# The opening of a two-block transformer on one core: raw input transposed and projected first, its norm factor applied to the sums

## The chip, the cores and the metric

The kernel runs on one NeuronCore of a Trainium2 chip. The metric is device microseconds of one execution, here the median of several. The core's engines work from queues of their own and wait for each other by semaphores: TensorE (PE: matrix products into PSUM; its weight loads are shown apart as PEld), VectorE (DVE), ScalarE (ACT), GpSimd (POOL) and SyncE (SP, which here only issues transfers). An engine takes its instructions strictly in the order in which the program gives them.

## The reference, cut to what matters

Two blocks follow one another on 256 tokens of width 1024. The first begins with a norm and one wide projection, and the change lies wholly in these lines:

```
def rmsnorm(x, g):
    xf = x.astype(jnp.float32)
    y = xf * lax.rsqrt(jnp.mean(xf * xf, axis=-1, keepdims=True) + EPS)
    return (y * g.astype(jnp.float32)).astype(x.dtype)
...
h = rmsnorm(x, norm_mix_g[l])
proj = h @ w_in[l]
cb, cc, ch, sq, sk, sv, rq, rk, rv, rg, gate_logits = jnp.split(proj, SPLIT_POINTS, axis=-1)
```

So each token (a row of x) has one factor, 1/sqrt(mean square + EPS), and each of the 1024 columns one gain g. sq, sk and sv (512 columns each) are query, key and value of a stick-breaking attention. All that follows (retention, gates, cross attention, two MLPs, an SSD mixer, an attention with latent keys) is the same program before and after.

## The kernel before

All products are exact to float32 by splitting. A value is rounded to a short part ("hi", type fp32r) and the rest ("lo" = value - hi), and a product is three matmuls: hi·hi, hi·lo, lo·hi. Weights come from memory in **units** of 128 x 2048 elements (1 MB) through five buffers. For each unit ACT makes `whi` from `raw` (helper `hi()`, L830), DVE makes `wlo` from both (helper `lo()`, L1310), and PE may begin a unit's third kind of product only when its `lo_split` count is reached; `weights(u)` (L2117 and after) waits for it at the unit's beginning. A buffer is loaded again when PE has finished the unit five places earlier. In this text unit 0 and unit 1 are the two halves of sq, unit 2 and unit 3 those of sk, unit 4 and unit 5 those of sv (each the product over one half of the 1024 inputs), and unit 6 is the first of the retention's. The places of `hi()` and `lo()` in ACT's and DVE's programs are written out by hand; nothing plans them at run time. PE's own order is unit after unit.

The opening before: SP loads token tile 0 of x and the two halves of unit 0; ACT loads tile 1, the identity matrix and the gains. DVE gets the mean square of tile 0 (bn_stats), ACT that of tile 1 (L871). GpSimd takes both to the power -0.5 (L742), DVE and ACT scale a tile each (L1531, L876) into `xs`, PE transposes it (L2286), and ACT and DVE make `h_hi` and `h_lo` from the transposed tile, times the gains (L864, L1364). PE fills the time until then with 20 products of zeros (L2325). It then runs `first_unit` (unit 0: hi·hi, L2295, then L2299 with `wlo`, L2304 with `h_lo`) and `second_unit` (unit 1), then unit 2 and so on (L2125 to L2127). Behind its `lo()` of unit 4 DVE computes the angles of a rotary table (L1548 to L1562) and zeroes two halves of the key buffers (L1564, L1565), and then takes the `lo()` of units 5, 6 and 7.

PSUM has eight banks; a bank is claimed by PE when its last content is `drained`.

Of the kernel before, what the change touches and what calls it, by code (L numbers as in the profile page):

```python
# [221 lines left out]
def plan(w):  # L222
# [4 lines left out]
    p.transposes("h1", 4, (4, 5, 6, 7))  # L227
    SQ, SK, SV, RET, CB, CC, CH, GATE = (MIX * j for j in (3, 4, 5, 6, 0, 1, 2, 10))
# [254 lines left out]
def build(nc, w, out):  # L483
# [3 lines left out]
    with ctx:  # L487
# [71 lines left out]
        squares, g_rows = room(6272, D), room(7552, P)[0:KD, :]  # L559
        xs = room(8320, NT, D)  # L560
# [48 lines left out]
        g_mix_in, squared = sem("g_mix_in"), sem("squared")  # L609
        x_scaled = [sem(f"x_scaled{t}") for t in range(NT)]  # L610
        first_in, first_hi, zeroed = sem("first_in"), sem("first_hi"), sem("zeroed")
        ms_ready, rstd_ready = sem("ms_ready"), sem("rstd_ready")
# [101 lines left out]
        def _(pool):  # L714
# [24 lines left out]
            pool.wait_ge(pool_step, 1)  # L739
            powers[0] += NT  # L740
            pool.wait_ge(ms_ready, NT)
            nc.gpsimd.tensor_tensor(rstd[:, 0:NT], ms[:, 0:NT], mhalf[:, 0:NT], ALU.pow).then_inc(rstd_ready, NT)  # L742
# [70 lines left out]
        def _(act):  # L813
# [53 lines left out]
            act.dma_start(xn[:, 1, :], w["x"][0].rearrange("(t p) n -> p t n", p=P)[:, 1, :]).then_inc(x_in[1], 16)  # L867
            act.dma_start(ident, w["constants"][:, C_IDENT:C_TRI]).then_inc(ident_in, 16)
            act.dma_start(g_rows, w["norm_mix_g"][0].rearrange("(k p) -> k p", p=P)).then_inc(g_mix_in, 16)
            act.wait_ge(x_in[1], 16)  # L870
# [9 lines left out]
            copy_bank(pv[:, G_MIX:G_MIX + KD], "g_mix", lambda b: b[:, 0:KD])  # L880
            wait_drained(act, "g_mix")
            for j in range(4):
                scaled_part_bank(h_hi[:, 2 * j:2 * j + 2, :], ("h1", j), G_MIX + 2 * j)
# [3 lines left out]
            for name in ("sq", "sk"):  # L887
                for j in range(2):
                    hi()
                    if name == "sq":  # L890
                        copy_bank(sqT[:, 2 * j:2 * j + 2, :], (name, j), pair)
                    else:
                        b = wait_bank(act, (name, j))
                        A(skT[0][0:64, 2 * j:2 * j + 2, :], pair(b)[0:64], ACT.Copy)
                        A(skT[1][64:P, 2 * j:2 * j + 2, :], pair(b)[64:P], ACT.Copy).then_inc(drained[use[(name, j)][0]], 1)
# [9 lines left out]
            for t in range(NT):  # L905
                copy_bank(svN[:, t, :], ("sv", t), lambda b: b[:, :])
# [384 lines left out]
        def _(dve):  # L1291
# [234 lines left out]
            dve.wait_ge(squared, 1)  # L1526
            V.tensor_scalar(ms[:, 1:2], msq[:, 1:2], 1.0 / D, RMS_EPS, ALU.mult, ALU.add).then_inc(ms_ready, 1)
            powers[0] += 1
            wait_inverse(NT)
            for c in halves:  # L1530
                V.tensor_scalar(xs[:, 0, c], xn[:, 0, c], rstd[:, 0:1], None, ALU.mult).then_inc(x_scaled[0], 1)  # L1531
# [6 lines left out]
            wait_drained(dve, "g_mix")  # L1538
# [26 lines left out]
            V.memset(skT[1][0:64, :, :], 0.0).then_inc(sk_zeroed, 1)  # L1565

# [542 lines left out]
        def _(pe):  # L2109
# [169 lines left out]
            def first_unit():  # L2279

                h1 = [claim(("h1", j)) for j in range(4)]
                for t in range(NT):
                    for k in range(KD):
                        if k % 4 == 0:
                            pe.wait_ge(x_scaled[t], k // 4 + 1)
                        last = nc.tensor.transpose(h1[k // 2][:, T * (k % 2) + P * t:T * (k % 2) + P * t + P], xs[:, t, P * k:P * k + P], ident)  # L2286
                        if t == 1 and k % 2:
                            last.then_inc(fill(("h1", k // 2)), 1)
                b = claim(("sq", 0))
                for k in range(KD):  # L2290
                    if k % 4 == 0:
                        pe.wait_ge(hi_split if k else first_hi, 1)
                    pe.wait_ge(x_hi, k + 1)
                    for c in range(2):
                        M(b[:, T * c:T * c + T], view(whi[0], KD, 256)[:, k, P * c:P * c + P], h_hi[:, k, :], start=(c, k) == (0, 0), stop=False)  # L2295
                w_hi, w_lo, _, _ = weights(at[("sq", 0)])
                for k in range(KD):
                    for c in range(2):
                        M(b[:, T * c:T * c + T], w_lo[:, k, P * c:P * c + P], h_hi[:, k, :], start=False, stop=False)  # L2299
                for k in range(KD):  # L2300
                    if k % 2 == 0:
                        wait_drained(pe, ("h1", k // 2))
                    for c in range(2):
                        last = M(b[:, T * c:T * c + T], w_hi[:, k, P * c:P * c + P], h_lo[:, k, :], start=False, stop=(c, k) == (1, KD - 1))  # L2304
                last.then_inc(unit_used, 1)

            def second_unit():
# [5 lines left out]
                for c in range(2):  # L2313
                    for k in range(KD):
                        for x_ in (h_hi, h_lo):
                            M(b[:, T * c:T * c + T], w_hi[:, k, P * c:P * c + P], x_[:, k, :], start=(c, k) == (0, 0) and x_ is h_hi, stop=False)
                _, w_lo, _, _ = weights(at[("sq", 1)])
                for c in range(2):
                    for k in range(KD):
                        last = M(b[:, T * c:T * c + T], w_lo[:, k, P * c:P * c + P], h_hi[:, k, :], start=False, stop=(c, k) == (1, KD - 1))  # L2320
# [3 lines left out]
            for _ in range(20):  # L2324
# [6 lines left out]
            second_unit()  # L2331
            for name in ("sq", "sk"):
                for j in range(2):
                    if name == "sk":
                        b_unit(at[(name, j)], h_hi, h_lo, one((name, j)))
# [11 lines left out]
            for k in range(2):  # L2347
                a_unit(at[("sv", k)], h_hi, h_lo, 4 * k, banks, k == 0, k == 1)


            pe.wait_ge(cst_a_in, 16)
# [633 lines left out]
```

## Time and profile before

| | us |
|---|---|
| median of 3 runs | 1258.52 (1258.48 to 1260.17) |
| span of the profiled execution | 1257.2 |
| PE busy | 1242.1 |
| DVE busy | 932.5 |
| ACT busy | 684.2 |
| POOL busy | 68.2 |

The span runs from the first to the last instruction of the profiled execution; the median of the timed runs is 1.3 us longer, as it holds what lies around the instructions. Matmuls overlap, so PE's pace is to be read from the distance of starts and not from the duration of one.

### The profile page before, as it was taken

The page shows a single profiled execution, that of the slowest core. Times are in us where ns is not written, and L with a number is a line of the kernel's source. Part 1 is how long each engine was busy: PE and PEld are TensorE (multiplying, and loading weights), DVE is VectorE, ACT ScalarE, POOL GpSimd, SP SyncE. Part 2 cuts the span into 40 slices and gives each one's busy share as a digit, 9 for nine tenths or more (in the row PEclk, how much of TensorE's full clock was granted, in tenths as well). Part 3 has the DMA queues.
Part 4 walks back from the last instruction along what each step waited for, and adds up shares of the span by engine and source line. Part 5 has one row for each costly group of instructions (what it writes and reads, how often), then busy time and mean ns, then how long its engine had stood idle before and what let it go on. Part 6 is the DMA issues. An engine that isn't in the chain of part 4 may idle for free. (4 is left out here: it accounts for less than half of the span.)

```text
span 1257.2 us, 18334 instructions
## 1 busy us (share of the span) xinstructions
PE 1242.1 (99%) x7514; PEld 1102.9 (88%) x7514; DVE 932.5 (74%) x1292; ACT 684.2 (54%) x872; POOL 68.2 (5%) x93
## 2 busy tenths in 40 slices
PE   9999999999999999999999999999999999999997
PEld 8878999989988888889998888888888888888886
DVE  6676857875456666577997998788888868788877
ACT  6654444343553444455777655466655574566652
POOL 2000000100000000000003331000000000000000
PEclk9999999999999999999999999999999999999999
DMA  9664545656435665647656654655554744655551
GB/s 294 219 184 144 185 143 188 214 186 209 168 101 170 199 194 178 197 138 219 185 168 210 203 191 151 217 185 201 184 186 138 231 134 134 201 194 179 197 194 41
DMA packets 162595, 227.97 MB, mean 181 GB/s; under 512 B 7853, under 2 KB 123825, under 8 KB 162384
## 3 DMA queue, kind: packets, MB, share of 16 engines
q1 hardware_dynamic: 159392, 216.68, 53.5%
q0 software_dynamic: 2816, 9.52, 2.3%
q8 instruction: 60, 0.98, 0.3%
q10 hardware_dynamic: 304, 0.59, 0.1%
q14 instruction: 23, 0.19, 0.0%
HBM read 225.68 MB, written 1.10 MB: 180 GB/s over the span
## 5 line engine op out<-in xcount | busy, mean ns | idle before, releaser
L1310 DVE TENSOR_TENSOR wlo<-raw,whi 128x2048 fp32r<-128x2048 f32 (+3 forms) x185 | 415.9, 2260 | 113.9 <-ACT whi L830 112.8
L830 ACT ACTIVATE whi<-raw 128x2048 fp32r<-128x2048 f32 (+3 forms) x185 | 345.9, 1883 | 16.0 <-DMA raw<-in_w_xkv 6.1
L2159 PE MATMUL psum<-h_both,whi 128*128 128x512 f32 x714 | 254.7, 396 | 0.0
L2158 PE MATMUL psum<-h_both,wlo 128*128 128x256 f32 x714 | 199.4, 279 | 0.3 <-DVE h_both L1364 0.3
L2125 PE MATMUL psum<-h_both,whi 128*128 128x256 f32 x688 | 195.9, 285 | 0.0
L2127 PE MATMUL psum<-h_both,wlo 128*128 128x256 f32 x688 | 194.6, 283 | 0.0
L2126 PE MATMUL psum<-h_both,whi 128*128 128x256 f32 x688 | 194.6, 283 | 0.0
L2125 PE MATMUL psum<-whi,r_hi 128*128 128x512 f32 x446 | 176.6, 396 | 0.0
L2127 PE MATMUL psum<-whi,r_lo 128*128 128x512 f32 x446 | 173.9, 390 | 0.0
L2126 PE MATMUL psum<-wlo,r_hi 128*128 128x512 f32 x446 | 173.8, 390 | 0.0
L2159 PEld LDWEIGHTS psum<-h_both,whi 128*128 128x128 f32 x714 | 134.0, 188 | 27.6
L2158 PEld LDWEIGHTS psum<-h_both,wlo 128*128 128x128 f32 x714 | 134.6, 189 | 5.2 <-DVE h_both L1364 0.6
L2125 PEld LDWEIGHTS psum<-h_both,whi 128*128 128x128 f32 x688 | 131.9, 192 | 0.4 <-issue 0.3
L2126 PEld LDWEIGHTS psum<-h_both,whi 128*128 128x128 f32 x688 | 131.9, 192 | 0.2
L2127 PEld LDWEIGHTS psum<-h_both,wlo 128*128 128x128 f32 x688 | 131.9, 192 | 0.0
L2125 PE MATMUL psum<-whi,h_both 128*128 128x512 f32 (+4 forms) x304 | 118.7, 391 | 0.4 <-issue 0.3
L1964 DVE SCALAR_TENSOR_TENSOR arena<-arena,pv 128x256 f32<-128x256 f32 x176 | 77.3, 482 | 51.7 <-ACT arena L1165 43.9
L2127 PE MATMUL psum<-whi,h_both 128*128 128x512 f32 (+4 forms) x304 | 113.5, 373 | 0.0
L2126 PE MATMUL psum<-wlo,h_both 128*128 128x512 f32 (+4 forms) x304 | 113.1, 372 | 0.0
L2127 PEld LDWEIGHTS psum<-whi,r_lo 128*128 128x128 f32 x446 | 83.7, 188 | 17.9
L2126 PEld LDWEIGHTS psum<-wlo,r_hi 128*128 128x128 f32 x446 | 83.9, 188 | 16.5
L2125 PEld LDWEIGHTS psum<-whi,r_hi 128*128 128x128 f32 x446 | 83.8, 188 | 15.3
(350 smaller groups left out, 1807.1 us busy)
## 6 DMA issues: line engine op xcount, KB each, us to landing
raw<-in_ffn_up SPq DMA_DIRECT2D x40, 1024.0 KB, 5.1
raw<-in_w_in SPq DMA_DIRECT2D x31, 1024.0 KB, 5.8
raw<-in_ssd_in_proj SPq DMA_DIRECT2D x22, 1024.0 KB, 5.4
raw<-in_ffn_down SPq DMA_DIRECT2D x22, 1024.0 KB, 4.9
raw<-in_w_up SPq DMA_DIRECT2D x16, 1024.0 KB, 5.6
raw<-in_w_down SPq DMA_DIRECT2D x16, 1024.0 KB, 4.9
raw<-in_w_xkv SPq DMA_DIRECT2D x8, 1024.0 KB, 5.2
raw<-in_ssd_out_proj SPq DMA_DIRECT2D x8, 1024.0 KB, 5.2
```

The lines of the kernel that those rows point to most:

```text
L830: A(whi[u % SLOTS][:, 0:kt * n], raw[u % SLOTS][:, 0:kt * n], ACT.Copy).then_inc(hi_split, 1)
L1310: V.tensor_tensor(wlo[s][:, 0:kt * n], raw[s][:, 0:kt * n], whi[s][:, 0:kt * n].bitcast(F32), ALU.subtract).then_inc(lo_split, 1)
L1964: ins = V.scalar_tensor_tensor(y, fpad[g % 2][x][:, ct, tap:tap + T], pv[:, wcol:wcol + 1], y, ALU.mult, ALU.add)
L2125: M(o, a_hi, b_hi, start=start, stop=False)
L2126: M(o, a_hi, b_lo, start=False, stop=False)
L2127: return M(o, a_lo, b_hi, start=False, stop=stop_)
L2158: M(b[:, 0:T], w_lo_k, h_hi[:, k, :], start=False, stop=False)
L2159: return M(b[:, :], w_hi_k, h_both[:, :, k, :], start=False, stop=k == kt - 1)
```

## The change

- SP loads both tiles of x, one behind the other, ahead of unit 0. ACT loads only the gains and the identity.
- PE transposes the **raw** x as soon as a tile is there (15 products of zeros ahead of it in place of 20), and ACT and DVE make `r_hi` and `r_lo` from it times the gains. sq, sk and sv (units 0 to 5) are computed from these un-normalized values.
- GpSimd rounds the first half of unit 0 (a copy of 128 x 1024), ahead of its constants' loads. The powers come behind eleven of its loads.
- DVE gets the mean squares of both tiles, tile 1's behind the `wlo` of unit 0. Behind `lo()` of unit 2 it makes two diagonal matrices of the tokens' factors. PE multiplies them with a matrix of ones, which gives `factor`, the factors along the free axis in all partitions. ACT copies it out of PSUM bank 2, which unit 2's sums claim next.
- DVE multiplies sq and sk by `factor` as it takes them out of PSUM (before: plain copies by ACT). ACT copies sv with the factor as its scale.
- The normalized h for all later projections is made beside this: DVE writes `xg` = transposed x times gain times factor, ACT rounds it to `h_hi`, DVE takes the rest, `h_lo`. PE waits for that behind unit 5 (`h1_lo`).

The diff, cut to its core:

```diff
 # SP
-            sp.dma_start(xn[:, 0, :], x_tiles[:, 0, :]).then_inc(x_in[0], 16)
+            for t in range(NT):
+                sp.dma_start(xn[:, t, :], x_tiles[:, t, :]).then_inc(x_in[t], 16)
...
 # GpSimd
-            pool.wait_ge(ms_ready, NT)
-            nc.gpsimd.tensor_tensor(rstd[:, 0:NT], ms[:, 0:NT], mhalf[:, 0:NT], ALU.pow).then_inc(rstd_ready, NT)
+            nc.gpsimd.memset(ones, 1.0).then_inc(pool_step, 1)
+            pool.wait_ge(first_in, 16)
+            nc.gpsimd.tensor_copy(whi[0][:, 0:UNIT // 2], raw[0][:, 0:UNIT // 2]).then_inc(first_hi, 1)
...
                 pool.dma_start(pvraw[r0:r0 + src.shape[0], blk, :], src).then_inc(pv_in, 16)
+            pool.wait_ge(pool_step, 2)
+            rsqrt_tiles()
...
 # ACT
-            A(squares, xn[:, 1, :], ACT.Square, accum_out=msq[:, 1:2]).then_inc(squared, 1)
-            act.wait_ge(first_in, 16)
-            A(whi[0][:, 0:UNIT // 2], raw[0][:, 0:UNIT // 2], ACT.Copy).then_inc(first_hi, 1)
-            act.wait_ge(rstd_ready, NT)
-            for c in range(2):
-                A(xs[:, 1, 512 * c:512 * c + 512], xn[:, 1, 512 * c:512 * c + 512], ACT.Copy, scale=rstd[:, 1:2]).then_inc(x_scaled[1], 1)
+            copy_bank(pv[:, G_MIX:G_MIX + KD], "g_mix", lambda b: b[:, 0:KD])
+            wait_drained(act, "g_mix")
+            for j in range(4):
+                scaled_part_bank(r_hi[:, 2 * j:2 * j + 2, :], ("h1", j), G_MIX + 2 * j)
             act.wait_ge(landed[0], 16)
             A(whi[0][:, UNIT // 2:], raw[0][:, UNIT // 2:], ACT.Copy).then_inc(hi_split, 1)
...
                     hi()
...
+                    if (name, j) == ("sq", 1):
+                        copy_bank(factor, "factor", lambda b: b[:, 0:T])
                     if (name, j) == ("sk", 1):
+                        for i in range(4):
+                            wait_drained(act, ("h1", i))
+                            part(h_hi[:, 2 * i:2 * i + 2, :], xg[:, 2 * i:2 * i + 2, :])
...
 # DVE
+            dve.wait_ge(x_in[1], 16)
+            norm_tile(1, xn, RMS_EPS, True)
+            lo()
+            lo()
+            for t in range(NT):
+                wait_inverse(t + 1)
+                V.tensor_scalar(factor_diag[:, P * t:P * t + P], ident, rstd[:, t:t + 1], None, ALU.mult).then_inc(diag_ready, 1)
+            lo()
+            wait_drained(dve, "factor")
+            both_tiles = lambda p0, p1: factor[p0:p1].unsqueeze(1).to_broadcast([p1 - p0, 2, T])
+            for j in range(2):
+                b = wait_bank(dve, ("sq", j))
+                V.tensor_tensor(sqT[:, 2 * j:2 * j + 2, :], pair(b), both_tiles(0, P), ALU.mult).then_inc(done(("sq", j)), 1)
             for j in range(4):
-                scaled_part_bank(h_lo, h_hi, ("h1", j), 2 * j, G_MIX + 2 * j)
+                b = bank[use[("h1", j)][0]]
+                for ct in range(2):
+                    k = 2 * j + ct
+                    ins = V.scalar_tensor_tensor(xg[:, k, :], b[:, T * ct:T * ct + T], pv[:, G_MIX + k:G_MIX + k + 1], factor, ALU.mult, ALU.mult)
+                ins.then_inc(done(("h1", j)), 1)
             lo()
-            for _ in range(3):
-                lo()
+            for j in range(4):
+                part(h_lo[:, 2 * j:2 * j + 2, :], xg[:, 2 * j:2 * j + 2, :], h_hi[:, 2 * j:2 * j + 2, :]).then_inc(h1_lo, 1)
...
             V.memset(skT[1][0:64, :, :], 0.0).then_inc(sk_zeroed, 1)
+            for j in range(2):
+                b = wait_bank(dve, ("sk", j))
+                V.tensor_tensor(skT[0][0:64, 2 * j:2 * j + 2, :], pair(b)[0:64], both_tiles(0, 64), ALU.mult)
+                V.tensor_tensor(skT[1][64:P, 2 * j:2 * j + 2, :], pair(b)[64:P], both_tiles(64, P), ALU.mult).then_inc(done(("sk", j)), 1)
 
             for _ in range(3):
                 lo()
...
 # PE
-            for _ in range(20):
+            for _ in range(15):
                 M(bank[7][:, 0:P], zeros, zeros, start=True, stop=True)
...
+            pe.wait_ge(diag_ready, 2)
+            pe.wait_ge(pool_step, 2)
+            b = claim("factor")
+            M(b[:, 0:T], ones, factor_diag, start=True, stop=True).then_inc(fill("factor"), 1)
```

In units 0 to 5 PE reads `r_hi`, `r_lo` where it read `h_hi`, `h_lo`, and `first_unit` takes the product with `r_lo` ahead of the one with `wlo`.

DVE's queue from the `lo()` of unit 1 on. Before (the x4 are units 1 to 4, the x3 units 5 to 7; CAST to the second MEMSET is the angle table and the zeroing):

```order
L1310 TENSOR_TENSOR wlo<-raw,whi 128x2048 x4
L1548 CAST pos_f<-pos_i 128x2
L1550 TENSOR_SCALAR ang<-cst,pos_f 128x32 x2
...
L1564 MEMSET arena 64x1024
L1565 MEMSET arena 64x1024
L1310 TENSOR_TENSOR wlo<-raw,whi 128x2048 x3
```

After, the same stretch of DVE's queue:

```order
L1306 TENSOR_TENSOR wlo<-raw,whi 128x2048 x2
L1544 TENSOR_SCALAR arena<-cst,rstd 128x128 x2
L1306 TENSOR_TENSOR wlo<-raw,whi 128x2048
L1550 TENSOR_TENSOR arena<-psum,arena 128x512 x2
L1555 SCALAR_TENSOR_TENSOR arena<-psum,pv,arena 128x256 x8
L1306 TENSOR_TENSOR wlo<-raw,whi 128x2048
L1340 TENSOR_TENSOR h_both<-arena,h_both 128x512 x4
L1564 CAST pos_f<-pos_i 128x2
...
L1584 TENSOR_TENSOR arena<-psum,arena 64x512
L1585 TENSOR_TENSOR arena<-psum,arena 64x512
L1584 TENSOR_TENSOR arena<-psum,arena 64x512
L1585 TENSOR_TENSOR arena<-psum,arena 64x512
L1306 TENSOR_TENSOR wlo<-raw,whi 128x2048 x3
```

Eighteen operations (2 + 8 + 4 + 4, beside the two small diagonals) now stand between the `lo()` of unit 3 and that of unit 5. PE's queue between its second and third unit, before and then after, where L2342 is unit 1's last part, L2357 the product for `factor` and L2145 unit 2:

```order
L2320 MATMUL psum<-h_both,wlo 128x256 x16
L2125 MATMUL psum<-h_both,whi 128x256
```

```order
L2342 MATMUL psum<-r_hi,wlo 128x256 x16
L2357 MATMUL psum<-arena 128x256
L2145 MATMUL psum<-r_hi,whi 128x256
```

One product with two waits (DVE's diagonals, GpSimd's ones) came in between.

## Rows read from the trace of the kernel before

**Rows 1.** The page: busy time and share of each engine; granted clock in tenths.
```profile
PE 1242.1 (99%) x7514; PEld 1102.9 (88%) x7514; DVE 932.5 (74%) x1292; ACT 684.2 (54%) x872; POOL 68.2 (5%) x93
...
PEclk9999999999999999999999999999999999999999
```

**Rows 2.** Waits of PE: waiting line, releaser, us in total, times, longest.
```profile
PE psum L2239 <- DVE xn L1481: 1.9, 4, 0.9
PE psum L2286 <- DVE arena L1531: 1.2, 1, 1.2
```

**Rows 3.** Timeline of PE's opening: start, us, operation, count, idle before.
```profile
1.06 6.46 PE L2325 MATMUL psum<-arena 128*128 128x128 f32 x40 [1.06 <-DVE arena L1523]
...
8.90 1.97 PE L2286 MATMUL psum<-cst,arena 128*128 128x128 f32 x16 [1.23 <-DVE arena L1531]
...
16.10 2.08 PE L2304 MATMUL psum<-h_both,whi 128*128 128x256 f32 x16
...
23.78 0.28 PE L2125 MATMUL psum<-h_both,whi 128*128 128x256 f32 x1
```

**Rows 4.** Timeline of ACT and DVE in the opening.
```profile
10.77 3.03 ACT L864 ACTIVATE h_both<-psum,pv 128x256 fp32r<-128x256 f32 x8
...
11.85 3.22 DVE L1364 SCALAR_TENSOR_TENSOR h_both<-psum,pv,h_both 128x256 fp32r<-128x256 f32 x8
```

**Rows 5.** Timeline of ACT: rounding of units 2 and 3 and what it waited for.
```profile
18.54 1.91 ACT L830 ACTIVATE whi<-raw 128x2048 fp32r<-128x2048 f32 x1 [2.94 <-DMA raw<-in_w_in]
...
21.80 1.92 ACT L830 ACTIVATE whi<-raw 128x2048 fp32r<-128x2048 f32 x1 [0.86 <-DMA raw<-in_w_in]
```

**Rows 6.** Timeline of DVE from unit 2 to unit 5.
```profile
20.49 2.29 DVE L1310 TENSOR_TENSOR wlo<-raw,whi 128x2048 fp32r<-128x2048 f32 x1 [2.56 <-ACT whi L830]
23.75 2.29 DVE L1310 TENSOR_TENSOR wlo<-raw,whi 128x2048 fp32r<-128x2048 f32 x1 [0.97 <-ACT whi L830]
26.46 2.29 DVE L1310 TENSOR_TENSOR wlo<-raw,whi 128x2048 fp32r<-128x2048 f32 x1 [0.42 <-ACT whi L830]
28.67 0.16 DVE L1548 CAST pos_f<-pos_i 128x2 f32<-128x2 int32 x1
...
35.30 2.22 DVE L1310 TENSOR_TENSOR wlo<-raw,whi 128x2048 fp32r<-128x2048 f32 x1
...
51.37 4.49 DVE L1310 TENSOR_TENSOR wlo<-raw,whi 128x2048 fp32r<-128x2048 f32 x2
```

**Rows 7.** Timeline of PE: first matmul of unit 4, first of unit 5, two 256-column products.
```profile
35.74 0.47 PE L2125 MATMUL psum<-whi,h_both 128*128 128x512 f32 x1
...
41.31 0.39 PE L2125 MATMUL psum<-whi,h_both 128*128 128x512 f32 x1
...
46.75 0.60 PE L2361 MATMUL psum<-arena 128*128 128x256 f32 x2
```

**Rows 8.** DVE and POOL by line and shape: count, busy us, mean ns, idle before.
```profile
L1693 DVE TENSOR_TENSOR arena<-psum,arena 128x512 f32<-128x512 f32 x12 | 8.2, 685 | 1.3 <-issue 1.0 <-DVE arena L1693 0.2
L1344 DVE TENSOR_TENSOR r_lo<-arena,r_hi 128x512 fp32r<-128x512 f32 x6 | 4.1, 691 | 1.6 <-ACT r_hi L846 1.4
L1741 DVE TENSOR_SCALAR arena<-arena,rinv 128x256 f32<-128x256 f32 x8 | 2.5, 351 | 0.1
L787 POOL TENSOR_TENSOR arena<-arena,cst 128x256 f32<-128x256 f32 x15 | 15.6, 1051 | 22.5 <-DMA arena<-decay_rows 22.3
```

**Rows 9.** Timeline of POOL: the power, the first and the last of its loads.
```profile
7.62 0.70 POOL L742 TENSOR_TENSOR rstd<-ms,mhalf 128x2 f32<-128x2 f32 x1 [6.77 <-DVE ms L1527]
8.27 0.71 POOL L754 DMA_DIRECT2D cst<-in_constants  x1
...
13.09 1.65 POOL L756 DMA_DIRECT2D arena<-in_ffn_conv_w  x3
```

**Rows 10.** PE in stretches: us, busy (instructions touching it), granted clock, DMA share, GB/s.
```profile
4.50:5.00 0.50, 0.50 (x5) 1.00 0.99 402
5.00:5.50 0.50, 0.50 (x7) 1.00 0.97 339
```

More of the change, by code:

```diff
@@ L227, in plan @@
     p.transposes("h1", 4, (4, 5, 6, 7))
+    p.small("factor", 2)
     SQ, SK, SV, RET, CB, CC, CH, GATE = (MIX * j for j in (3, 4, 5, 6, 0, 1, 2, 10))
@@ L558, in build @@
         memN = room(8320, NT, D)
-        squares, g_rows = room(6272, D), room(7552, P)[0:KD, :]
-        xs = room(8320, NT, D)
+        xg = room(6272, KD, T)
+        g_rows = room(8320, P)[0:KD, :]
+        factor, factor_diag, ones = room(8448, T), room(8704, T), room(8960, P)
         zeros = room(0, P)
@@ L879, in _ @@
             nxt[0] += 1
[L880 to L883, printed above, removed]
             hi()
@@ L1525, in _ @@
             norm_tile(0, xn, RMS_EPS, True)
[L1526 to L1531, printed above, removed]
+            wait_drained(dve, "g_mix")
+            for j in range(4):
+                b = wait_bank(dve, ("h1", j))
+                parts[0] += 2
+                dve.wait_ge(x_hi, parts[0])
+                for ct in range(2):
+                    k = 2 * j + ct
+                    ins = V.scalar_tensor_tensor(r_lo[:, k, :], b[:, T * ct:T * ct + T], pv[:, G_MIX + k:G_MIX + k + 1],
+                                                 r_hi[:, k, :].bitcast(F32), ALU.mult, ALU.subtract)
+                ins.then_inc(raw_lo, 1)
             for i, half_rounded in enumerate((first_hi, hi_split)):
@@ L2289, in first_unit @@
                 b = claim(("sq", 0))
+                w_hi = view(whi[0], KD, 256)
                 for k in range(KD):
-                    if k % 4 == 0:
-                        pe.wait_ge(hi_split if k else first_hi, 1)
+                    if k == 0:
+                        pe.wait_ge(first_hi, 1)
+                    if k == KD // 2:
+                        pe.wait_ge(hi_split, 1)
                     pe.wait_ge(x_hi, k + 1)
                     for c in range(2):
-                        M(b[:, T * c:T * c + T], view(whi[0], KD, 256)[:, k, P * c:P * c + P], h_hi[:, k, :], start=(c, k) == (0, 0), stop=False)
-                w_hi, w_lo, _, _ = weights(at[("sq", 0)])
+                        M(b[:, T * c:T * c + T], w_hi[:, k, P * c:P * c + P], r_hi[:, k, :], start=(c, k) == (0, 0), stop=False)
+                for k in range(KD):
+                    if k % 2 == 0:
+                        pe.wait_ge(raw_lo, k // 2 + 1)
+                    for c in range(2):
+                        M(b[:, T * c:T * c + T], w_hi[:, k, P * c:P * c + P], r_lo[:, k, :], start=False, stop=False)
+                _, w_lo, _, _ = weights(at[("sq", 0)])
                 for k in range(KD):
                     for c in range(2):
[L2299 to L2304, printed above, removed]
+                        last = M(b[:, T * c:T * c + T], w_lo[:, k, P * c:P * c + P], r_hi[:, k, :], start=False, stop=(c, k) == (1, KD - 1))
                 last.then_inc(unit_used, 1)
@@ L2314, in second_unit @@
                     for k in range(KD):
-                        for x_ in (h_hi, h_lo):
-                            M(b[:, T * c:T * c + T], w_hi[:, k, P * c:P * c + P], x_[:, k, :], start=(c, k) == (0, 0) and x_ is h_hi, stop=False)
+                        for x_ in (r_hi, r_lo):
+                            M(b[:, T * c:T * c + T], w_hi[:, k, P * c:P * c + P], x_[:, k, :], start=(c, k) == (0, 0) and x_ is r_hi, stop=False)
                 _, w_lo, _, _ = weights(at[("sq", 1)])
@@ L2334, in _ @@
                     if name == "sk":
-                        b_unit(at[(name, j)], h_hi, h_lo, one((name, j)))
+                        b_unit(at[(name, j)], r_hi, r_lo, one((name, j)))
                     if (name, j) == ("sk", 1):
@@ L2347, in _ @@
             for k in range(2):
-                a_unit(at[("sv", k)], h_hi, h_lo, 4 * k, banks, k == 0, k == 1)
+                a_unit(at[("sv", k)], r_hi, r_lo, 4 * k, banks, k == 0, k == 1)
+            pe.wait_ge(h1_lo, 4)
             pe.wait_ge(cst_a_in, 16)
```

30 lines of the change are left out of this document (11 added, 19 removed).

## The prediction, made before the changed kernel was run

> **What bounds the kernel now.** I read the page first. PE is busy for 1242.1 of 1257.2 us, at the full granted clock in all 40 slices, and no other engine comes near [rows 1]. So the time is the length of PE's queue plus the places where PE stands. The view of PE's waits says how few these are: the longest entries are 1.9 us in all for the first transposes of later blocks and 1.2 us for those of the opening [rows 2]. From the opening on PE runs without a gap. An edit to the opening therefore has exactly two ways to move the end: it can start PE's unbroken stream earlier, or it can tear a hole into it. I look for both, in the order of PE's queue, and the number that counts is the start of a fixed matmul far enough behind the edited stretch.
>
> PE's timeline [rows 3] has the opening: products of zeros until 7.5, transposes from 8.90, unit 0's last part from 16.10 to about 18.0, unit 2 from 23.78. Unit 0's first part there is paced by ACT, which writes eight parts of `h_hi` in 3.03 us; DVE writes `h_lo` beside it in 3.22 [rows 4].
>
> Behind it the other engines are nearly as tight as PE, and this is what the change has to be measured against. ACT rounded units 2 and 3 only when their transfers landed, at 18.54 and 21.80, after idle times of 2.94 and 0.86 us [rows 5]. DVE follows at once: units 2, 3 and 4 at 20.49, 23.75 and 26.46, then the angle table and the zeroing from 28.67 to 35.30, then unit 5 from 35.30 to 37.5 [rows 6]. PE begins unit 4 at 35.74 and unit 5 at 41.31 [rows 7]. So DVE has unit 5 ready 41.31 - 37.52 = 3.8 us ahead of PE, and it stood idle only 0.42 us between the unit 3 and unit 4 of that chain. Anything above 3.8 + 0.4 = 4.2 us that is put into DVE's queue between unit 3 and unit 5 makes PE wait for unit 5.
>
> **Part 1: the opening proper.** Raw x can be transposed when it lands, without the power and the scaling. Products of zeros: 15 in place of 20. The first records come at five in half a microsecond, then at seven [rows 10], so the five that go are quick ones: 10 of 40 records at about 0.115 us, 1.15 us. PE reaches the transposes at about 6.4 in place of 8.90. They take 2.0 us; ACT's eight parts (3.03) can start when the first bank is whole, at about 7.5, and end at 10.5. But ACT rounds the second half of unit 0 only behind them, 1.05 us more, 11.6, and PE needs that for its last eight matmuls of the first part: these end at 12.6. Then 16 with `r_lo` and 16 with `wlo` at 0.12 us, 1.92 each: unit 0 ends at 16.4 in place of 18.0. DVE in the meantime: `r_lo` to 11.6, two halves of `wlo` at 1.2 to 13.9, tile 1's mean square 1.9 to 15.8, unit 1 to 18.1, in time for PE (20.3). Gain so far 1.6 us.
>
> GpSimd's rounding of the half unit has no row. The nearest is its addition on 128 x 256 elements at 1051 ns [rows 8]; four times that is 4.2 us, and ACT's speed for the same shape, 1.06, is the other end. Loaded at about 7.3 it is done between 8.4 and 11.5. PE needs it 1 us ahead of 11.6, DVE at 11.6: between nothing and 0.9 us here, and nothing at the end, since the next part takes back more than that. The Trainium skill (GPSIMD Engine Reference, 4.1 Engine selection) calls one-input work there "roughly line-rate", which would be near the short end; no run here shows it, and the sum stays the same.
>
> GpSimd's power moves behind the constants and eleven small loads: these were 8.27 to 14.74 [rows 9], 6.5 us. From 8.4 to 11.5 they end at 15 to 18, and two powers at 0.8 each make 16.5 to 19.6. DVE asks for them at 22.8, so they cost nothing, with at least 3 us to spare.
>
> **Part 2: the factor takes the gain back.** Unit 2's arrival is set by the memory stream, which has the same bytes in the same order; its `wlo` is ready at 22.8 as before. Then come two diagonals of 128 x 128. The nearest row is 351 ns for 128 x 256 [rows 8]; I take 0.2 each, 0.4 to 0.7 for both: 23.2. PE has been through unit 1 since 22.3 and waits. Its product for `factor` is float32 on 256 columns like L2361, 0.44 from start to start [rows 7]: 23.75. Unit 2 claims the same bank, and ACT has to copy it out first, about 0.5 with hand-over. Unit 2 starts at 24.4, 0.6 us later than the 23.78 of before. The 1.6 us are gone, and a little more.
>
> **Part 3: DVE's queue up to unit 5.** This carries the forecast. A DVE instruction behind another starts 0.09 us before the first one's end: two of 2.29 take 4.49 [rows 6]. So I take the mean less 0.09. Behind unit 3, which still starts at 23.75 as ACT still waits for its landing, and ends at 25.95 by starts:
> - sq times factor, 2 x 128x512 from PSUM: like L1693, 0.685 [rows 8]: 2 x 0.60 = 1.2
> - `xg`, 8 x 128x256 from PSUM: as the eight of `h_lo` in 3.22 [rows 4], 0.39 each: 3.1
> - unit 4: 2.2
> - `h_lo`, 4 x 128x512: L1344 on SBUF inputs, 0.691 [rows 8]: 4 x 0.60 = 2.4
> - angle table and zeroing, as before: 35.30 - 28.67 = 6.6 [rows 6]
> - sk times factor, 4 x 64x512: partitions do not shorten it, so 4 x 0.60 = 2.4
> - unit 5: 2.2, to 46.15 in all.
>
> The additions are 9.1 us against room for 4.2. PE, from 24.4, gets through units 2, 3, the small transposes and unit 4 in the 17.5 us that it took before (41.31 - 23.78), and is at unit 5 at 41.9. It waits until 46.2, some 4.3 us. Unit 5 starts at 46.25 in place of 41.31: **4.9 us later**. As DVE's chain and not PE's sets this point, all that parts 1 and 2 do drops out of the sum.
>
> What else is late? ACT's parts of `h_hi` are ready for DVE (unit 5 of the weights lands by about 28, parts from 29 to 31.5, wanted from 32.6). Behind unit 5 DVE does units 6 and 7 by 50.6, wanted by PE at 52.2 and 57.8; after that DVE waited for ACT until 51.37 anyway, so it is level again. PE has no slack to give back in the later blocks, so the 4.9 us stay to the end: 1257.2 + 4.9 = 1262.1 of span, and with the 1.3 us between that span and the median 1258.52 + 4.9, **1263.4**.
>
> **Rivals.**
> *The clock falls in the pause.* The longest pauses of PE behind its first product are 1.2 and 0.9 us [rows 2], so it cannot say what a pause of 4.3 us does. The opening shows what a cold start costs: the clock's column reads 1.00, but the records come five in half a microsecond until 5.0 and seven after, which I read as 3.9 us (from 1.06 on) at the lower of the two levels, 1.2 GHz for 2.4 [rows 10], half of which is lost, 2 us. The same behind the pause gives 1265.4. The Trainium skill (TensorE: Matmul & The Clock Gate, Part 1: The HAM clock gate) has TensorE throttled to half rate after it stood idle and released by activity; the trace's opening agrees, a mid-kernel fall no row shows.
> *A shorter queue.* GpSimd's loads, 0.6 MB, begin up to 3 us later, and if units 2 and 3 land that much earlier, up to 1.5 us, DVE's chain moves with them: 1262 to 1263. Against it: their bytes were all moved before unit 3 landed in either order.
> *Not slower: the opening's gain arrives.* The point from which this decides is 4.2 us of additions. DVE would have to do the eighteen operations in less than half of their rows' time, or reach them earlier. Then only PE's part stands: with unit 2's stream as it is +0.6, 1259.1; with unit 2 landing 1.6 us earlier and the diagonals with it, -1.0, 1257.5.
> *GpSimd is slow, the powers are late.* Decides from 22.8 on: a rounding of over 7 us. Each further microsecond moves the diagonals, and DVE's whole queue, by one: 1265 and above.
>
> **How the numbers follow.** Forecast 0.50 (1262.7 to 1264.3); clock 0.25 (1264.5 to 1266.5); shorter queue 0.12 (1261 to 1262.7); not slower 0.08 (1257 to 1261); late powers 0.05. The range of 8 in 10 takes in the first three, without the far end of the clock's: 1261.0 to 1266.3. About 0.2% (2.5 us) is what a measurement of this kernel can tell from no change; faster than that 0.03, within it 0.07, slower 0.90.
>
> **What the profile will show.** Right: transposes near 6.4; unit 0 done near 16.4; a pause of PE ahead of unit 2 with DVE's diagonals as releaser; PE idle for about 4.3 us ahead of unit 5's first matmul at about 46.2, released by DVE's `wlo`. Wrong in part 3: the eighteen operations taking under 5 us, or DVE idle between them. Wrong in part 1: GpSimd's copy over 4 us. The forecast as a whole is wrong if PE has no gap between 25 and 50, or if a later stall of before is shorter by as much.

## The result, and the profile after

The changed kernel takes 1267.7 us (1266.4 to 1268.7, three runs) where the kernel before took 1259.4 (1258.5 to 1260.4, four runs): slower by a ratio of 1.0067, 95% interval 1.0054 to 1.0080. A fourth run of the changed kernel took 2051.2 us at a mean granted clock of 0.556, where the three have 0.994 to 0.996, and is left out. The forecast was 1263.4, with a range of 1261.0 to 1266.3, so the time lies above the range. The direction and the place were right; the loss is 8.4 us and not 4.9.

The page of the changed kernel: busy time by engine, and the granted clock in 40 slices. PE is busy for 3 us more than in [rows 1], and the second slice of the clock reads 8 where it read 9:

```profile
span 1265.9 us, 18341 instructions
...
PE 1245.1 (98%) x7506; PEld 1104.6 (87%) x7506; DVE 941.7 (74%) x1314; ACT 679.9 (54%) x866; POOL 75.1 (6%) x96
...
PEclk9899999999999999999999999999999999999999
```

Its waits of PE, against [rows 2]. The first and the third are new: the wait for unit 5's `wlo`, and one in the opening for ACT's second half of unit 0. The wait for the bank of `factor` is there too:

```profile
PE psum L2145 <- DVE wlo L1306: 4.0, 1, 4.0
PE psum L2259 <- DVE xn L1477: 2.1, 5, 0.9
PE psum L2317 <- ACT whi L878: 1.9, 1, 1.9
...
PE psum L2145 <- ACT arena L858: 0.6, 1, 0.6
```

PE's timeline, against [rows 3] and [rows 7] (start, us, operation, count, idle before):

```profile
6.33 1.97 PE L2305 MATMUL psum<-cst,xn 128*128 128x128 f32 x16
8.70 1.21 PE L2317 MATMUL psum<-r_hi,whi 128*128 128x256 f32 x8 [0.41 <-POOL whi L744]
11.77 2.08 PE L2317 MATMUL psum<-r_hi,whi 128*128 128x256 f32 x8 [1.85 <-ACT whi L878]
...
23.66 0.59 PE L2357 MATMUL psum<-arena 128*128 128x256 f32 x2
24.82 0.36 PE L2145 MATMUL psum<-r_hi,whi 128*128 128x256 f32 x1 [0.56 <-ACT arena L858]
...
46.53 0.80 PE L2145 MATMUL psum<-whi,r_hi 128*128 128x512 f32 x1 [3.96 <-DVE wlo L1306]
47.12 0.63 PE L2146 MATMUL psum<-wlo,r_hi 128*128 128x512 f32 x1
47.55 0.63 PE L2147 MATMUL psum<-whi,r_lo 128*128 128x512 f32 x1
...
54.76 0.60 PE L2388 MATMUL psum<-arena 128*128 128x256 f32 x2
```

Unit 2 starts at 24.82 (23.78 before), unit 5 at 46.53 (41.31), and the two-key product behind unit 5 at 54.76 (46.75). So 1.0 us are lost by unit 2, 5.2 by unit 5, and 8.0 behind it: unit 5 itself took 8.2 us in place of 5.4. Nothing waits in it. Its matmuls stand 0.43 us apart where they stood 0.23 apart, as the clock is at the lower level until 52. The stretches of PE (us, length, busy time with the number of instructions, granted clock, DMA share, GB/s):

```profile
11.00:12.00 1.00, 0.23 (x1) 0.60 1.06 338
12.00:13.00 1.00, 1.00 (x5) 0.50 1.04 273
...
40.00:45.00 5.00, 2.56 (x12) 1.00 0.60 184
45.00:50.00 5.00, 3.47 (x8) 0.53 0.43 160
50.00:52.00 2.00, 2.00 (x6) 0.50 0.00 0
52.00:54.00 2.00, 2.00 (x10) 0.96 0.00 0
```

1.00 is 2.4 GHz and 0.50 is 1.2. It fell in both pauses: after 11 us, behind PE's products in the opening (back between 14 and 15), and at 45.3, inside the wait for unit 5, where it stayed low until 52.2, 6.8 us. The Trainium skill (TensorE: Matmul & The Clock Gate, Part 1: The HAM clock gate) says that an idle array is brought down to half rate and only released by activity; these rows agree, with 1.2 GHz behind both pauses.

DVE's queue after, against [rows 6]: unit 3, sq times factor, `xg`, unit 4, `h_lo`; then, behind the angle table, the last of sk times factor and units 5 to 7:

```profile
23.63 2.29 DVE L1306 TENSOR_TENSOR wlo<-raw,whi 128x2048 fp32r<-128x2048 f32 x1 [0.32 <-ACT whi L834]
25.84 1.28 DVE L1550 TENSOR_TENSOR arena<-psum,arena 128x512 f32<-128x512 f32 x2
27.04 3.22 DVE L1555 SCALAR_TENSOR_TENSOR arena<-psum,pv,arena 128x256 f32<-128x256 f32 x8
30.17 2.28 DVE L1306 TENSOR_TENSOR wlo<-raw,whi 128x2048 fp32r<-128x2048 f32 x1
32.37 2.49 DVE L1340 TENSOR_TENSOR h_both<-arena,h_both 128x512 fp32r<-128x512 f32 x4
...
41.40 0.62 DVE L1584 TENSOR_TENSOR arena<-psum,arena 64x512 f32<-64x512 f32 x1
...
44.18 6.69 DVE L1306 TENSOR_TENSOR wlo<-raw,whi 128x2048 fp32r<-128x2048 f32 x3
```

DVE is idle twice between 25.84 and 44.18, for 0.28 and 0.27 us at the zeroing, as in the kernel before; the forecast's 6.6 us for table and zeroing hold both. Unit 5's `wlo` starts at 44.18, forecast 43.9.

### The profile page after: what moved, and what is told of

The parts are those of the page before. It is cut to its first block and busy times, and to the rows that moved or that the text cites. A ratio compares the mean times of both kernels' runs of the same rounds, so it can differ in the third digit from the quotient of the medians.

```text
span 1265.9 us, 18341 instructions
## 1 busy us (share of the span) xinstructions
PE 1245.1 (98%) x7506; PEld 1104.6 (87%) x7506; DVE 941.7 (74%) x1314; ACT 679.9 (54%) x866; POOL 75.1 (6%) x96
## 5 line engine op out<-in xcount | busy, mean ns | idle before, releaser
L2178 PE MATMUL psum<-h_both,wlo 128*128 128x256 f32 x714 | 199.4, 279 | 0.3 <-DVE h_both L1360 0.3
L2145 PE MATMUL psum<-whi,r_hi 128*128 128x512 f32 x462 | 184.3, 399 | 4.0 <-DVE wlo L1306 4.0
L2145 PE MATMUL psum<-h_both,whi 128*128 128x256 f32 x656 | 186.8, 285 | 0.0
L2147 PE MATMUL psum<-h_both,wlo 128*128 128x256 f32 x656 | 185.6, 283 | 0.0
L2146 PE MATMUL psum<-h_both,whi 128*128 128x256 f32 x656 | 185.5, 283 | 0.0
L2147 PE MATMUL psum<-whi,r_lo 128*128 128x512 f32 x462 | 181.1, 392 | 0.0
L2146 PE MATMUL psum<-wlo,r_hi 128*128 128x512 f32 x462 | 180.9, 392 | 0.0
L2179 PEld LDWEIGHTS psum<-h_both,whi 128*128 128x128 f32 x714 | 134.0, 188 | 27.6
L2178 PEld LDWEIGHTS psum<-h_both,wlo 128*128 128x128 f32 x714 | 134.6, 189 | 5.2 <-DVE h_both L1360 0.6
L2145 PEld LDWEIGHTS psum<-h_both,whi 128*128 128x128 f32 x656 | 125.8, 192 | 0.4 <-issue 0.3
L2146 PEld LDWEIGHTS psum<-h_both,whi 128*128 128x128 f32 x656 | 125.8, 192 | 0.2
L2147 PEld LDWEIGHTS psum<-h_both,wlo 128*128 128x128 f32 x656 | 125.8, 192 | 0.0
L1984 DVE SCALAR_TENSOR_TENSOR arena<-arena,pv 128x256 f32<-128x256 f32 x176 | 77.3, 481 | 51.7 <-ACT arena L1161 43.9
L2145 PE MATMUL psum<-whi,h_both 128*128 128x512 f32 (+4 forms) x288 | 112.4, 390 | 0.8 <-issue 0.7
L2147 PE MATMUL psum<-whi,h_both 128*128 128x512 f32 (+4 forms) x288 | 107.2, 372 | 0.0
L2146 PE MATMUL psum<-wlo,h_both 128*128 128x512 f32 (+4 forms) x288 | 106.9, 371 | 0.0
L2145 PEld LDWEIGHTS psum<-whi,r_hi 128*128 128x128 f32 x462 | 87.5, 189 | 20.6 <-DVE wlo L1306 4.4
```

What stands on the lines that cost most here:

```text
L1984: ins = V.scalar_tensor_tensor(y, fpad[g % 2][x][:, ct, tap:tap + T], pv[:, wcol:wcol + 1], y, ALU.mult, ALU.add)
L2145: M(o, a_hi, b_hi, start=start, stop=False)
L2146: M(o, a_hi, b_lo, start=False, stop=False)
L2147: return M(o, a_lo, b_hi, start=False, stop=stop_)
L2178: M(b[:, 0:T], w_lo_k, h_hi[:, k, :], start=False, stop=False)
L2179: return M(b[:, :], w_hi_k, h_both[:, :, k, :], start=False, stop=k == kt - 1)
```

## Experiments

**Theory:** the length of DVE's queue makes the hole ahead of unit 5, and the hole makes the clock fall; both cost. **Rivals:** the loss comes with something else in the change (the raw operands, the moved transfers); or the clock's fall is chance and the pause is all. The ratios compare with runs of the kernel before on the same chip, three chips in all: one for experiments 1 and 2 and for 2 and 4 additions in experiment 3, one for 3 additions, `a_nofill` and `a_best12`, one for the rest.

### 1. Unit 5 taken early

The changed kernel, with DVE's `lo()` of unit 5 directly behind `h_lo`, ahead of the angle table:

```diff
                 part(h_lo[...], xg[...], h_hi[...]).then_inc(h1_lo, 1)
+            lo()
...
-            for _ in range(3):
+            for _ in range(2):
                 lo()
```

> The changed kernel with DVE's wlo of unit 5 taken directly behind h_lo, ahead of the angle table, the zeroing and sk times factor. Theory (DVE's queue makes the hole, the hole makes the clock fall): DVE has unit 5 at about 37.1, PE arrives at it at 42.3 (unit 2 starts at 24.8, plus 17.5) and does not wait, the granted clock stays at full speed from 15 us on. What is left is unit 2's late start, 24.8 for 23.8, so +1.0 us on the kernel before, and up to 0.3 more at unit 6, which DVE then reaches at 48.7 where PE wants it at 48.4: about +1.0 to +1.5 us in all. Rival (the loss comes with the un-normalized operands or the moved transfers and not with the order of DVE's queue): still +7 us or more.

Measured 1262.8 against 1259.2, ratio 1.0027 (1.0017 to 1.0037). The 4 us wait ahead of unit 5 is gone; the only wait for a `wlo` that is left is unit 2's:

```profile
PE psum L2146 <- DVE wlo L1306: 0.6, 1, 0.6
```

The product behind unit 5 stands at 49.10 (46.75 before, 54.76 changed), and the clock is full from 20 us to that point:

```profile
26.05 0.36 PE L2146 MATMUL psum<-r_hi,whi 128*128 128x256 f32 x1 [0.57 <-DVE wlo L1306]
...
49.10 0.60 PE L2389 MATMUL psum<-arena 128*128 128x256 f32 x2
```

More than half of the loss (8.4 against 3.6 us) goes with one moved instruction: it was the order of DVE's queue. The rival, +7 us or more, is out. But 3.6 us are left and not 1.0 to 1.5. The profiled run was one of the longer ones of the nine, 1.1 us above their median. Of its 4.9 us of span, 2.35 are there by 49 us: unit 2 starts at 26.05, 2.3 late, since the opening ran at half rate from 13.3 to 16.7 and its products of zeros had ended a microsecond later than in the other trace. The other large piece comes 900 us later, at the transposes between the layers of the second block, where PE also stands for 0.7 and 0.9 us before:

```profile
983.46 0.66 PE L2260 MATMUL psum<-cst,xn 128*128 128x128 f32 x4 [0.69 <-DVE xn L1477]
984.98 0.66 PE L2260 MATMUL psum<-cst,xn 128*128 128x128 f32 x4 [0.86 <-DVE xn L1477]
...
986.00:987.00 1.00, 1.00 (x3) 0.54 0.42 98
```

There the clock fell in this run and not in the traces of before and of the changed kernel, although PE stands there in these too. So part of what separates single runs arises far behind the edited stretch.

### 2. The pause filled with work

The changed kernel, with 16 products of the identity with itself on PE ahead of unit 5:

```diff
             for k in range(2):
+                if k == 1:
+                    pe.wait_ge(drained[5], 1)
+                    for _ in range(16):
+                        M(bank[5][:, 0:P], ident, ident, start=True, stop=True)
                 a_unit(at[("sv", k)], r_hi, r_lo, 4 * k, banks, k == 0, k == 1)
```

> The changed kernel with 16 products of the identity with itself on PE, into a free bank, ahead of unit 5: PE works through the pause, about 3.7 of its 4.0 us, and waits as long for the weights. Theory (of the 8.4 us lost, 5.2 are the wait and 2.8 the lower clock behind it): unit 5 still starts at about 46.5, 5.2 us later than before, but the clock stays at full speed and unit 5 takes 5.4 in place of 8.2 us: about +5.3 to +5.8 us on the kernel before. Rival (the clock's fall has nothing to do with the pause, or its cost is covered by something else): +8 us as measured for the change.

```profile
43.49 3.73 PE L2377 MATMUL psum<-cst 128*128 128x128 f32 x32
...
47.27 0.50 PE L2145 MATMUL psum<-whi,r_hi 128*128 128x512 f32 x1
...
52.87 0.60 PE L2392 MATMUL psum<-arena 128*128 128x256 f32 x2
```

Unit 5 took 52.87 - 47.27 = 5.6 us and not 8.2, at full clock: in this trace the mechanism is as the theory says. The time, 1266.8 against 1259.2 (+7.6), ratio 1.0061 (1.0049 to 1.0074), is above the 5.3 to 5.8 us expected. Of the 7.8 us of the profiled run's span, 6.0 are there at unit 5's start and 6.1 behind it. The start is 0.7 later than in the first trace because DVE's chain is: its `lo()` of unit 3 began at 24.37 (23.63 there), that of unit 5 at 44.92 (44.18), and was done at 47.2. The other 1.7 us came later; where from was not looked into. By the times alone the two theories are not apart: +7.6 is nearer to the rival's +8 than to 5.8. What speaks for the theory is the trace.

### 3. Idle additions in DVE's queue of the kernel before

The kernel before, with additions whose result nothing uses, behind DVE's `lo()` of unit 4 (here four):

```diff
             for _ in range(3):
                 lo()
+            for _ in range(4):
+                chain(V.tensor_tensor(rows[:, :, :], xn[:, :, :], xn[:, :, :], ALU.add))
```

> The kernel before, with 4 additions of 128 x 2048 on DVE between unit 4's wlo and the angle table, with nothing that uses their result: 4 x 2.33 = 9.3 us, as much as the change's eighteen operations. Theory (only the length of this queue counts): room is 3.8 + 0.4 us, so PE waits 9.3 - 4.2 = 5.1 us ahead of unit 5, the clock falls in the pause as in the changed kernel and costs 2.8 more: about +8 us. Rival (the pause alone does not bring the clock down, it needs the weaker opening or another cause too): +5 us.

> The same with 2 additions, 4.7 us. Theory (a threshold at 4.2 us): PE waits 0.5 us ahead of unit 5, the clock stays: +0.5 us. Rival (what is put into DVE's queue costs as it is, without room): +4.7 us.

> The kernel before with 3 idle additions on DVE, 7.0 us, between those with 2 (a wait of 1.3 us, no fall of the clock) and 4 (a wait of 6.0, clock low for 6.8 us). Theory (room of 3.4 to 4.2 us, then each microsecond is a microsecond of wait, and the clock comes on top where the pause is long enough): a wait of 3.6 us ahead of unit 5; the clock falls in most runs, for 3.4 us or more, 1.7 us lost: +3.6 where it stays, +5.3 where it falls. Rival (the clock falls in proportion to the pause): always the same time, near +4.5.

| additions | angle table starts later by | wait ahead of unit 5 | time against before | ratio |
|---|---|---|---|---|
| 2 | 5.2 us | 1.3 us | +1.2 | 1.0009 (1.0000 to 1.0018) |
| 3 | 7.0 us | 3.0 us | +3.2, +3.4, +4.9, +6.9, +7.5 | 1.0042 (1.0028 to 1.0056) |
| 4 | 10.0 us | 6.0 us | +7.7 | 1.0057 (1.0042 to 1.0073) |

PE's wait ahead of unit 5 in the traces with 2, then 4 additions:

```profile
PE psum L2126 <- DVE wlo L1310: 1.3, 1, 1.3
```

```profile
PE psum L2126 <- DVE wlo L1310: 6.0, 1, 6.0
```

With 4, everything of the opening as it was, the old kernel loses nearly what the change loses (7.7 against 8.4), and its clock falls in the same place (stretches of PE):

```profile
45.00:46.00 1.00, 0.00 (x0) 0.98 1.03 403
46.00:47.00 1.00, 0.00 (x0) 0.50 0.28 105
...
52.00:53.00 1.00, 1.00 (x4) 0.61 0.00 0
```

Unit 5 takes 8.0 us there in place of 5.4. So neither raw operands nor moved transfers are needed. The room is 5.2 - 1.3 = 3.9 us with 2 additions, 7.0 - 3.0 = 4.0 with 3 and 10.0 - 6.0 = 4.0 with 4: the 3.8 us of the prediction. The expectation for 2 was half a microsecond, for two reasons too little. It counted with a room of 4.2, but the 0.4 us in which DVE was idle lie ahead of unit 4, and these additions stand behind it. And the two took the 4.6 us that I had priced (29.21 to 33.85); the other 0.5 of the 5.2 is that DVE came to unit 4 that much later, at 27.00 in place of 26.46, as it had to wait longer for ACT's rounding of unit 3.

With 3 additions the trace shows a pause of 3.0 us and no fall; its runs fall into two groups, +3.2 to +3.4 with a mean clock of 0.999 and +4.9 to +7.5 with 0.995 to 0.997. I read this as a pause that brings the clock down in some runs and not in others; where it fell in the runs without a trace is not recorded. The rival, the same time in every run near +4.5, is out.

### 4. The changed kernel once more

> The changed kernel once more, unaltered, for more runs beside those of the experiments. Theory: the loss is 5.2 us of PE's later start at unit 5 and 2 to 3 us of lower clock behind the pause, which comes every time since the pause is 4 us long: 1266.4 to 1268.7 again, no run below 1265. Rival (the fall of the clock behind the pause is chance): runs near 1264 among them.

1267.6 (1266.3 to 1268.6) against 1258.7, ratio 1.0069 (1.0057 to 1.0082); no run below 1266. That alone does not show a fall of the clock in each, as the runs of experiment 2 took 1266.3 to 1268.1 too. In this trace PE waited for 2.8 us only, as its opening was a microsecond later:

```profile
46.46 0.50 PE L2145 MATMUL psum<-whi,r_hi 128*128 128x512 f32 x1 [2.82 <-DVE wlo L1306]
...
53.63 0.60 PE L2388 MATMUL psum<-arena 128*128 128x256 f32 x2
```

The clock fell later than in the first trace, not in the pause but at 47.0, half a microsecond after PE had begun again, and was back at 50.5 (stretches of PE):

```profile
46.00:47.00 1.00, 0.54 (x2) 1.00 0.98 342
47.00:48.00 1.00, 1.00 (x4) 0.52 1.02 399
```

Unit 5 starts at the same moment as in the first trace, 46.5, although unit 2 started at 25.9 and not 24.8: DVE's chain sets this point, as forecast. Unit 5 takes 7.2 us: 8.2, 7.2 and, in experiment 2, 5.6, by how long the clock was low while PE worked on it.

### 5. The opening's clock, and a mended version

`a_u5_open` is experiment 1 with eight products of the identity in the opening's pause. `a_best` has in addition the diagonals behind unit 1's `wlo` in place of unit 2's, `factor` in bank 3 in place of 2, and the zeroing on GpSimd (told here, not in the diff). `a_nofill` is `a_best` without the eight products, `a_best_loads` is `a_best` with GpSimd's twelve loads (the constants and eleven small ones) behind its powers, `a_best12` is `a_best` with 12 products of zeros ahead in place of 15.

```diff
 # PE, first_unit (a_u5_open)
                     if k == KD // 2:
+                        for _ in range(8):
+                            M(bank[2][:, 0:P], ident, ident, start=True, stop=True)
                         pe.wait_ge(hi_split, 1)
...
 # plan and DVE (a_best)
-    p.small("factor", 2)
+    p.small("factor", 3)
...
             lo()
-            lo()
             for t in range(NT):
                 wait_inverse(t + 1)
                 V.tensor_scalar(factor_diag[...], ident, rstd[:, t:t + 1], None, ALU.mult).then_inc(diag_ready, 1)
             lo()
+            lo()
```

> The changed kernel with unit 5's wlo early, as in the experiment on that, and 8 products of the identity on PE between the two halves of unit 0's first part, where PE stands 1.9 us and the clock fell at 11.2 for 3.4 us. Theory (the opening's gain was eaten by this fall as well): the clock stays at full speed, unit 0 ends at 16.6 and not at 17.9 to 19.1, PE waits for the diagonals of the factor then, and unit 2 starts at 24.3: 1 us below the experiment without the filling, about 1261.5. Rival (the opening's clock does not matter, as unit 2 hangs on DVE's and the memory's side): no difference to that experiment, 1262.8.

> As the last one, and in addition: the factor's two diagonals behind unit 1's wlo in place of unit 2's, the factor in PSUM bank 3 (which unit 3 claims) in place of bank 2 (unit 2), and the zeroing of the two key buffers on GpSimd in place of DVE. Theory: PE computes the factor without a wait at 22.3 and starts unit 2 at 22.9 to 23.2, when its wlo is there, 0.7 us earlier than the kernel before; DVE has unit 6 at 46.4, as PE wants it. The time is 0.5 to 1 us below the kernel before, 1258.4. Rival (another wait takes the place, DVE's at unit 6 above all): above the kernel before by 1 us or more, with a wait of PE between 45 and 50.

> As the last one, with GpSimd's two powers ahead of its twelve loads (0.6 MB), which so start at 16.5 in place of 8.6. Theory (memory bounds the arrival of unit 2): units 2 and 3 land 1 to 1.8 us earlier, DVE has unit 2 at 21.5 and PE itself bounds, unit 2 starts at 22.8; 0.1 to 0.4 us below the last one. Rival (these loads are hidden, the stream of weights is bounded otherwise): unit 2's rounding on ACT still waits until 18.5 and nothing changes.

> The mended kernel (unit 5's wlo early, early diagonals, the factor in bank 3, zeroing on GpSimd) without the 8 products of the identity in the opening. Theory (a pause of 1.9 us there, with 16 of the first products thinly spread, brings the clock down for 3.4 us just before unit 0 and unit 1): unit 0 ends 1.3 us later, unit 2 starts at 23.5 to 24.5, 1 us above the mended kernel, 1261. Rival (the memory side bounds unit 2 anyway): the same 1260.2.

> The mended kernel with 12 products of zeros in place of 15. In the runs so far PE left these at 6.2 to 7.4 us, by when the clock had risen (4 to 6.7 us), and everything in the new opening followed it. Theory (the raw opening is the first that lies bare to this): with 12 PE is free at 6.1 in the late case too and waits for the identity instead; unit 0 ends up to 1 us earlier in those runs, none in the others: 0.5 us less in the median, 1259.7, and nearer to each other. Rival (fewer products keep the clock down for longer): the transposes run at the low level and the time is the same or above.

| kernel | median | before beside it | ratio |
|---|---|---|---|
| a_u5_open | 1261.7 | 1258.7 | 1.0025 (1.0017 to 1.0034) |
| a_best | 1260.2 | 1258.7 | 1.0016 (1.0007 to 1.0025) |
| a_best_loads | 1260.2 | 1258.7 | 1.0010 (1.0001 to 1.0019) |
| a_nofill | 1262.3 | 1259.2 | 1.0023 (1.0014 to 1.0032) |
| a_best12 | 1260.1 | 1259.2 | 1.0006 (0.9998 to 1.0015) |

`a_nofill` and `a_best` differ by the eight idle products: 3.1 and 1.6 us above before, on two chips and with intervals that overlap. Beside `a_nofill` on one chip stands `a_best12`, 2.2 us faster, but that also has three products of zeros fewer. And `a_u5_open` was to be 1 us below experiment 1 by these products; the ratios, 1.0025 and 1.0027, show no difference. So the times speak for the filling without settling it; the traces show what it does. In `a_nofill` the second half of the first part waits and the sixteen products with `r_lo` take 2.72 us, the clock being at the lower level from 12.1 to 15.5; in `a_best` it stays at the full level and they take 2.08:

```profile
12.19 2.07 PE L2321 MATMUL psum<-r_hi,whi 128*128 128x256 f32 x8 [1.91 <-ACT whi L883]
14.06 2.72 PE L2326 MATMUL psum<-r_lo,whi 128*128 128x256 f32 x16
```

```profile
12.02 1.21 PE L2323 MATMUL psum<-r_hi,whi 128*128 128x256 f32 x8
13.07 2.08 PE L2328 MATMUL psum<-r_lo,whi 128*128 128x256 f32 x16
...
46.07 0.60 PE L2394 MATMUL psum<-arena 128*128 128x256 f32 x2
```

In `a_u5_open` a wait of 0.7 us at unit 6 came up, as DVE was behind there; the zeroing on GpSimd took it away. In the trace of `a_best` the product behind unit 5 stands at 46.07, 0.7 us **ahead** of the kernel before, and DVE's last scaling starts at 1252.46 in place of 1253.36, 0.9 ahead. So the opening's gain is there in this profile, once nothing takes it back. In the time it is not: 1258.4 was expected and 1260.2 measured, and the profiled run was the fastest of the eleven. The span of that execution is 1257.4, that of before 1257.2: behind DVE's last instruction SP waited 2.8 us for the last store, and 1.7 before:

```profile
SPq L488 <- DMA out<-xn: 2.8, 1, 2.8
```

```profile
SPq L487 <- DMA out<-xn: 1.7, 1, 1.7
```

All four versions with the zeroing on GpSimd wait 2.8 us there; the changed kernel, experiment 2 and `a_u5_open` wait 1.8, experiment 1 2.2. One packet of 8 KB on the instruction queue went out in the last microseconds of each of these traces, and none in before's. It cannot be the packet as such, which stands beside the shorter waits as well; it went out between 2.5 and 3 us ahead of the end there, before the wait began, and in the four between 1.5 and 2, inside it. Whether that holds up the store is open. Why the median of `a_best` is 1.0 us above its profiled run is open too: its runs go from 1259.2 to 1262.1, before's from 1258.1 to 1260.0.

The new opening follows the clock's rise, as PE has to be done with its products of zeros: in the traces with 15 of them the transposes start between 6.3 and 7.6. The old one waited for the power anyway: its start is between 8.90 and 9.06 in the traces of before and of experiment 3, whether these products ended at 7.5 or at 8.5. With 12 of them the identity's transfer sets the start in this trace. The median is 0.9 above before in place of 1.6, but the two intervals overlap, so this gain is not shown:

```profile
6.09 0.22 PE L2357 MATMUL psum<-cst,arena 8*128 8x8 f32 x1 [0.28 <-DMA cst<-in_constants]
...
45.75 0.60 PE L2394 MATMUL psum<-arena 128*128 128x256 f32 x2
```

Moving GpSimd's loads did what was expected of the stream, and nothing to the time (1260.2 both). ACT's roundings of units 2 and 3:

```profile
15.84 1.92 ACT L839 ACTIVATE whi<-raw 128x2048 fp32r<-128x2048 f32 x1 [1.43 <-DMA raw<-in_w_in]
18.96 1.92 ACT L839 ACTIVATE whi<-raw 128x2048 fp32r<-128x2048 f32 x1 [1.21 <-DMA raw<-in_w_in]
```

They stand at 17.78 and 21.05 in `a_best`. So 0.6 MB of loads do delay the weights, by 2 us.

None of these beats the kernel before. `a_best12` is level with it, within the measurement.

## Where the prediction was right, and the step that failed

The profiled spans differ by 8.7 us: 5.2 by unit 5's later start, 2.8 by the clock in unit 5, 0.7 far behind. The sum had 4.9 for the first and nothing for the others. The forecast time lay another 0.8 us low because it stood on a median of 1258.5 for the kernel before, which is 1259.4 beside the result.

**DVE's queue (part 3): right.** Forecast: unit 5 at 46.25 on PE, 4.9 us late, after a wait of 4.3. Measured: 46.53, 5.2 late, 4.0. By term: sq 1.2 (forecast 1.2), `xg` 3.1 (3.1), `h_lo` 2.4 (2.4), sk 44.18 - 41.40 = 2.8 (2.4). The four operations on half the partitions start 0.70 apart and not 0.60. Idle additions to the old kernel gave a room of 3.9 to 4.0 us for the 3.8. That parts 1 and 2 drop out of the sum was right for unit 5 (experiment 4).

**The clock behind the pause: the step that failed.** The sum counted the pause of PE at its length and put the slow stretch behind it at nothing; the fall of the clock was named only as a rival, at 0.25 and 2.0 us. In its place both traces of the changed kernel show the clock at 1.2 GHz while PE works on unit 5, once from inside the pause and once from just behind it. That costs 8.23 - 5.44 = 2.8 us in the first trace and 7.17 - 5.44 = 1.7 in the second. All eight runs lose 7.0 us or more, above the 5.2 of the later start; as experiment 2 shows, their times alone do not say that it was the clock in each. The chance was too low, for want of any pause that long in the old trace. The price of 2.0 lies between the two that were measured: I took the opening's 3.9 us at the low level as the length of it, and it was low for 6.8 us in the first trace, partly inside the pause, and for 3.4 in the second.

**Part 1: right on the work, wrong on the clock.** Transposes at 6.33 (forecast 6.4); GpSimd's copy 1.04 us, at the fast end of 1.06 to 4.2; the wait for ACT's second half ended at 11.77 (11.6). But unit 0 ended at 17.9, not 16.4: PE had 8 matmuls between 8.3 and 11.8 and the clock fell there too, at 11.2, for 3.4 us. I had looked for a pause's effect on the clock only ahead of unit 5, and not in the pause of part 1 that I had worked out myself.

**Part 2: right in kind, 0.4 us short.** Forecast 24.4, measured 24.82: with unit 0 late PE reached the factor's product at 23.66, when the diagonals had been there for 0.4 us. PE waited for the bank as forecast, 0.56 us. But the sign that the prediction named, a pause with DVE's diagonals as releaser, did not come: between units 1 and 2 PE waited for ACT's copy alone.

**The other rivals** did not come. The queue was not shorter, since unit 3's rounding still started at 21.7. That rival was hardly put to the test: GpSimd's copy was quick, so its loads began at 8.59 and not up to 3 us after the 8.27 of before. When they were really late (`a_best_loads`), units 2 and 3 did land 2 us earlier, against what the prediction argued. The powers were there at 18.65, well ahead of 22.8. The remaining 0.7 us of the profiled span (8.0 behind unit 5, 8.7 at the end) came 700 us and more behind the change and differ from run to run; what sets them was not looked into.

## What to carry to other kernels

Before work is moved onto an engine that is "74% busy", count the slack at the next thing that the bound engine takes from it: here 3.8 us, and everything above it was paid in full. A new operation belongs behind the deliveries that others wait for, not ahead of them; one `lo()` moved ahead of the angle table gave back more than half of the loss. And a pause of the matmul engine of a few microseconds is to be priced with the slow stretch behind it (here 1.7 to 2.8 us where the clock fell), in every pause that the new schedule has, the opening's own among them.

## What the runs showed of the hardware

- A copy of 128 x 1024 float32 to fp32r took GpSimd 1.04 us, as fast as ACT's 1.06 and a quarter of the 4.2 that its addition's rate would give.
- PE's one wait ahead of unit 5 and the clock, by trace: 1.3 us, no fall; 2.8, a fall just behind it, low for 3.4 us; 3.0, no fall; 4.0, a fall, low for 6.8; 6.0, a fall, low for 6.8.
- GpSimd's power on one column took 0.59 us beside short DVE operations and 2.53 beside a DVE subtraction with two SBUF inputs (15.96 to 18.25), ending 0.4 us behind it; 0.59 and 2.53 again in `a_best`. The Trainium skill (SBUF — State Buffer, Who interferes with whom) says that such a DVE operation holds the read port that GpSimd shares; the rows agree:

```profile
15.15 0.59 POOL L729 TENSOR_TENSOR rstd<-ms,mhalf 128x1 f32<-128x1 f32 x1
16.12 2.53 POOL L729 TENSOR_TENSOR rstd<-ms,mhalf 128x1 f32<-128x1 f32 x1 [0.38 <-DVE ms L1401]
```

- The clock rises at different moments of the opening, read from the distance of PE's records as the clock's column shows 1.00 there: in the eight traces with 15 products of zeros, these ended between 6.2 and 7.5 us. A schedule that starts real work at once makes this spread its own.
